# A gate vector cut in two around the out-projection, one set of square sums for two norms, and last slots by blocks of rows

## The chip, the cores and the metric

The kernel runs on one core of a Trainium2 chip. The metric is the device time of one execution in microseconds (us). The clocks in the profile are granted clocks of TensorE, as a share of 2.4 GHz: 1.00 is 2.4 GHz and 0.50 is 1.2 GHz.

## What is computed

Two transformer blocks in a row on one sequence of 256 tokens of width 1024, all in float32.

```python
def first_block(x, c, ...):
    cond = silu(c)
    for l in range(2):
        mod = cond @ w_ada[l] + b_ada[l]
        sh1, sc1, g1, sh2, sc2, g2 = split(mod, 6)
        h = rms_norm(x, g_norm_mix[l]) * (1 + sc1) + sh1
        z = h @ w_in[l]
        a_out = dsa_mixer(...)                    # sparse attention, 6 heads
        b_out = hgrn2_mixer(..., hgrn_out_norm)   # recurrence, norm per head, silu gate
        c_out = gmlp_mixer(...)                   # spatial products
        x = x + g1 * (concatenate([a_out, b_out, c_out]) @ w_out[l])
        h = rms_norm(x, g_norm_ffn[l]) * (1 + sc2) + sh2
        y = swiglu(h, ...) if l == 0 else moe_swiglu(h, ...)   # 8 experts, 2 per token
        x = x + g2 * y
    return rms_norm(x, g_final)

def second_block(x, ...):
    h = x + forgetting_attention(rms_norm_2(x, a_norm), ...)
    h = h + conv_ffn(rms_norm_2(h, f_norm[0]), ...)
    kv = shared_kv(h, ...)
    h = h + native_sparse_attention(rms_norm_2(h, b_norm), kv, ...)
    return h + conv_ffn(rms_norm_2(h, f_norm[1]), ...)
```

## The kernel before

**Weights.** SyncE (SP) streams all large weights in one fixed order, `ORDER`, through a ring of six buffers `raw` of 1 MB (L709). A slot is loaded when the slot six before it has been used. ScalarE copies a slot into `w_hi`, rounded (`split`, L877), and VectorE takes the rest into `w_lo` (L1853). TensorE makes three products for each one wanted: high by high, low by high and high by low (`three`, L1256 to L1258). ScalarE and VectorE run a few slots ahead of TensorE. The conditioning weights `ada` are the exception: TensorE uses them unsplit.

**Conditioning vectors.** Each of the twelve vectors takes four slots and 16 products on one row (`vector`, L1298), a row copy with its bias by ScalarE (`vec_row`, L1065), a broadcast over the partitions by TensorE (`over_rows`, L1308), and for most a copy into `mod` (`vec_over_rows`, L1073, counted by `vec_made`). In the order of use of a layer they are: scale and shift of the first norm, gate of the mixers (`first`), scale (`first + 1`) and shift (`first + 2`) of the second norm, and the gate of the FFN or of the experts (`6 * l + 5`). Bias rows come from GpSimd's (POOL's) queue (`next_bias`).

**Order.** Each engine has its own instruction stream, written out by hand in the order of the computation, with semaphores between them. For a layer of the first block it is: norm, in-projection, index scores and top 64 on VectorE while TensorE makes the vectors; attention (`attend`); recurrence in eight levels; its output in two banks (signal `o_out`, L1660 to L1662); the gate vector `vector(6 * l + 5)`; the transposes of the spatial weights (L1668); the spatial products (L1675); transposes of `mix` (L1332); out-projection; norm; FFN or experts. ScalarE copies the transposed spatial weights (L1137) before it takes the root of the recurrence's norm (L956).

**Out-projections and down-projections.** A slot of an out-projection holds four chunks of the contraction for 512 columns. TensorE goes over the chunks and, for each, over the two blocks of 128 rows. When a group of 512 columns is complete, VectorE adds both blocks into `X` (`into_residual`, L1870, L1963, L1965). The last down-projection slot of a dense FFN is used in the same way (`dense`). `square_sums` (L951) on ScalarE squares each block of `X`, `inv_rms` and `norm_rows` make the normed rows `H` (L1933, L1936), TensorE transposes them, ScalarE copies the columns into `xT_hi` (L943) and VectorE makes `xT_lo` (L1903).

**Experts.** The sum over experts is in `acc`; for each expert `scatter` (L1518) puts the rows back by a product and `take` (L2158) adds them, weighted. After the last expert all four engines that need it read the overflow word (more than 128 rows for an expert) and branch. Then `add_gated` (L1870, L2240) adds `acc` times the gate to `X`; one norm with `g_final` writes `X` (L2504), and a second with `a_norm_2` writes `H`.

**Fillers.** `turns(n)` (L1315) issues n products on TensorE whose results nobody reads: 12 before the transposes that follow the experts, 4 in each convolution layer, 5 before the shared keys, 9 before the compressed keys. In a convolution layer TensorE first transposes the taps (L1748) and ScalarE copies them (L1198) before its squares.

**The end.** When both blocks of `X` are complete, VectorE signals with a small copy (`beat`, L2020), and SP stores `X` in one DMA (L760).

## Time and profile before

| what | value |
|---|---|
| median of 3 runs (lowest, highest) | 2475.71 us (2468.77, 2479.25) |
| profiled execution, its own time | 2482.26 us |
| its span, first to last instruction | 2480.2 us |
| TensorE products busy | 2331.4 us, 94% |
| VectorE busy | 1838.7 us, 74% |
| ScalarE busy | 1330.6 us, 54% |
| moved by DMA | 584.43 MB, mean 236 GB/s |
| mean granted clock | 0.95 |

A busy TensorE is not TensorE at its peak, since its products overlap and their ends are modelled. A row of the timeline reads: start, duration, engine, line, operation, what it writes and reads, how many instructions are merged in the row, and in brackets the idle time of the engine before it and what ended that idle time. What matters for a joint is which engine arrives last.

### The profile page before, as it was taken

The numbers are of one execution on the slowest core, as the hardware profiler recorded it, in microseconds if no ns is written. First come the engines' busy times: TensorE is split into PE (matmuls) and PEld (weight loads), VectorE is DVE, ScalarE is ACT, GpSimd is POOL, SyncE is SP. The second block draws the span as 40 slices with busy tenths as digits, with TensorE's granted clock in tenths as the row PEclk, the third lists the DMA queues.
The fourth block names the chain that finished last, engine by engine and source line by source line (L and its number), as shares of the span: only waits on it lengthen the run. The fifth ranks groups of instructions, "written<-read, shape, count | busy, mean of one in ns | idle before, by whom it ended". The sixth has DMA issues, their size and how long they took to land.

```text
span 2480.2 us, 30703 instructions
## 1 busy us (share of the span) xinstructions
PE 2331.4 (94%) x12633; PEld 1916.2 (77%) x12633; DVE 1838.7 (74%) x2231; ACT 1330.6 (54%) x1335; POOL 34.2 (1%) x62
## 2 busy tenths in 40 slices
PE   7979999988899999999999999997989999888998
PEld 4666999657578888888888888875768997656998
DVE  4746564675778888888988888875747887765886
ACT  3332543442467777677777777763444433464432
...
GB/s 345 234 111 186 196 187 187 198 268 43 156 298 352 365 350 365 352 360 355 362 354 361 353 362 355 361 347 100 157 32 180 186 184 131 135 1 84 185 185 101
DMA packets 281266, 584.43 MB, mean 236 GB/s; under 512 B 12014, under 2 KB 86876, under 8 KB 280992
## 3 DMA queue, kind: packets, MB, share of 16 engines
...
HBM read 581.32 MB, written 1.05 MB: 235 GB/s over the span
## 4 chain that ended last, share of the span: by engine, by line
PE 85%; DVE 8%; ACT 4%; DMA 2%; issue 1%; DVEq 0%; POOL 0%; ACTq 0%; POOLq 0%
PE ps L1256 24%; PE ps L1258 24%; PE ps L1257 24%; PE ps L1298 2%; DVE w_lo L1853 2%; PE ps L1362 1%; DMA raw<-in_w_ada 1%; PE ps L1377 1%; PE ps L1619 1%; PE ps L1400 1%; ACT arena L973 1%; PE ps L1477 1%; DVE arena L2061 1%; DVE arena L1870 1%; PE ps L1636 1%
## 5 line engine op out<-in xcount | busy, mean ns | idle before, releaser
L877 ACT ACTIVATE w_hi<-raw 128x2048 fp32r<-128x2048 f32 x500 | 948.7, 1906 | 435.0 <-PE ps L1258 317.0
L1853 DVE TENSOR_TENSOR w_lo<-raw,w_hi 128x2048 fp32r<-128x2048 f32 x500 | 1117.3, 2272 | 25.6 <-ACT w_hi L877 23.6
L1256 PE MATMUL ps<-w_hi,xT_hi 128*128 128x512 f32 (+1 forms) x1408 | 553.9, 393 | 14.0 <-DVE w_lo L1853 5.8
L1257 PE MATMUL ps<-w_lo,xT_hi 128*128 128x512 f32 (+1 forms) x1408 | 546.4, 388 | 0.0
L1258 PE MATMUL ps<-w_hi,xT_lo 128*128 128x512 f32 (+1 forms) x1408 | 546.3, 388 | 0.0
L1256 PEld LDWEIGHTS ps<-w_hi,xT_hi 128*128 128x128 f32 x1408 | 270.4, 192 | 69.3 <-issue 8.1
L1258 PEld LDWEIGHTS ps<-w_hi,xT_lo 128*128 128x128 f32 x1408 | 270.1, 192 | 54.0
L1257 PEld LDWEIGHTS ps<-w_lo,xT_hi 128*128 128x128 f32 x1408 | 270.8, 192 | 50.7
L1256 PE MATMUL ps<-xT_hi,w_hi 128*128 128x256 f32 x1056 | 299.7, 284 | 4.7 <-DVE xT_lo L1903 4.7
L1257 PE MATMUL ps<-xT_lo,w_hi 128*128 128x256 f32 x1056 | 299.4, 284 | 0.0
L1258 PE MATMUL ps<-xT_hi,w_lo 128*128 128x256 f32 x1056 | 299.4, 283 | 0.0
L1256 PE MATMUL ps<-w_hi,aT_hi 128*128 128x512 f32 (+1 forms) x744 | 287.3, 386 | 2.2 <-DVE aT_lo L2179 1.4
L1257 PE MATMUL ps<-w_lo,aT_hi 128*128 128x512 f32 (+1 forms) x744 | 287.1, 386 | 0.0
L1258 PE MATMUL ps<-w_hi,aT_lo 128*128 128x512 f32 (+1 forms) x744 | 286.8, 385 | 0.0
L1256 PEld LDWEIGHTS ps<-xT_hi,w_hi 128*128 128x128 f32 x1056 | 203.2, 192 | 7.1 <-DVE w_lo L1853 3.1
L1257 PEld LDWEIGHTS ps<-xT_lo,w_hi 128*128 128x128 f32 x1056 | 203.3, 193 | 1.1
L1258 PEld LDWEIGHTS ps<-xT_hi,w_lo 128*128 128x128 f32 x1056 | 203.2, 192 | 0.0
L1256 PEld LDWEIGHTS ps<-w_hi,aT_hi 128*128 128x128 f32 (+1 forms) x744 | 137.6, 185 | 30.9 <-DVE aT_lo L2179 1.7
L1258 PEld LDWEIGHTS ps<-w_hi,aT_lo 128*128 128x128 f32 (+1 forms) x744 | 137.4, 185 | 28.6
L1257 PEld LDWEIGHTS ps<-w_lo,aT_hi 128*128 128x128 f32 (+1 forms) x744 | 137.5, 185 | 27.2
L1041 ACT ACTIVATE aT_hi<-arena 128x512 fp32r<-128x512 f32 x33 | 20.9, 632 | 178.4 <-DVE arena L2141 178.4
L1298 PE MATMUL ps<-raw,small 128*64 128x512 f32 x384 | 91.4, 627 | 3.1 <-DMA raw<-in_w_ada 3.1
...
## 6 DMA issues: line engine op xcount, KB each, us to landing
raw<-in_moe_w_gate SPq DMA_DIRECT2D x112, 1024.0 KB, 5.9
raw<-in_moe_w_up SPq DMA_DIRECT2D x112, 1024.0 KB, 5.4
raw<-in_moe_w_down SPq DMA_DIRECT2D x112, 1024.0 KB, 5.7
raw<-in_w_ada SPq DMA_DIRECT2D x48, 1024.0 KB, 7.8
raw<-in_f_w_up SPq DMA_DIRECT2D x44, 1024.0 KB, 5.0
raw<-in_f_w_down SPq DMA_DIRECT2D x22, 1024.0 KB, 5.1
raw<-in_w_in SPq DMA_DIRECT2D x20, 1024.0 KB, 7.9
raw<-in_a_w_in SPq DMA_DIRECT2D x12, 1024.0 KB, 5.2
```

What stands on the lines that cost most here:

```text
L877: act.activation(w_hi[:, k % HI, 0:size], raw[:, r, 0:size], ACT.Copy).then_inc(ring.w_hi_ready, 1)
L973: last = act.activation(x, x, ACT.Exp, bias=negmax[:, s % 4, h:h + 1], accum_out=rowsum[:, s % 4, h:h + 1])
L1256: pe.matmul(out_, lh, rh, start=start, stop=False)
L1257: pe.matmul(out_, lh, rl, start=False, stop=False)
L1258: return pe.matmul(out_, ll, rh, start=False, stop=stop)
L1298: last = pe.matmul(out_[HD * s:HD * s + HD, :], condT[:, 2 * q + c:2 * q + c + 1].to_broadcast([P, HD]), w[:, c, s, :], start=q == 0 and c ...
L1362: last = pe.transpose(ps[0:kw, 6 + u // 4, (u % 4) * P:(u % 4 + 1) * P], bufs[at.nth[i] % 3][:, x:x + kw], ident)
L1377: last = pe.matmul(ps[:, 4 * (1 - s % 2) + h % 2, (h // 2) * 256:(h // 2) * 256 + W], q(h), k(h), start=True, stop=True)
L1400: last = pe.matmul(out_[:, j * P:j * P + w], v[0 if shared else 2 * j + parity](c), Ts[s % 2][0:kw, x:x + w], start=at.first[i] and c == 0 ...
L1477: last = pe.transpose(ps[:, 2, j * P:(j + 1) * P], e_act[:, j * P:(j + 1) * P], ident)
L1619: last = pe.matmul(ps[:, 2 * (level % 2) + u // 4, (u % 4) * P:(u % 4 + 1) * P], h_LF[:, b, u // 2 * P:(u // 2 + 1) * P], const[:, e:e + P ...
L1853: dve.tensor_tensor(w_lo[:, k % RAW, 0:size], raw[:, k % RAW, 0:size], w_hi[:, k % HI, 0:size].bitcast(F32), ALU.subtract).then_inc(ring.w ...
```

## The change

The stream order becomes: one slot of the gate vector of the FFN (or experts) ahead of the out-projection, its other three slots (`ada05_rest`, `ada15_rest`) behind it. On TensorE one quarter of that vector stands after the spatial products and three after the out-projection. The scale of the second norm is broadcast after the spatial weights' transposes, and the shift after the out-projection, where `norm_rows` reads it from PSUM. The recurrence's output is normed with fewer steps behind `o_out`. Last slots are used block of rows by block of rows, with the signal `first_block` between. In the experts, what is summed before the last expert is folded into `X` early, and the squares of `X` and of `X` times `g_final` give both norms. The store is made in two parts. The fillers are not touched.

```diff
+        FIRST_PART = 1
         def linears():
             s = {}
             for l in range(2):
                 for v in range(6):
-                    s[f"ada{l}{v}"] = [(2, D, rows(a["w_ada"][l], 2 * q, 2, v * D, D)) for q in range(KC // 2)]
+                    slots = s[f"ada{l}{v}"] = [(2, D, rows(a["w_ada"][l], 2 * q, 2, v * D, D)) for q in range(KC // 2)]
+                s[f"ada{l}5"], s[f"ada{l}5_rest"] = slots[:FIRST_PART], slots[FIRST_PART:]
...
-        ORDER = ["ada01", "ada00", "in0", "ada02", "ada04", "ada03", "ada05", "out0", "ada11", "ffn0", "ada10", "in1",
-                 "ada12", "ada14", "ada13", "ada15", "out1", "moe",
+        ORDER = ["ada01", "ada00", "in0", "ada02", "ada04", "ada03", "ada05", "out0", "ada05_rest", "ada11", "ffn0", "ada10", "in1",
+                 "ada12", "ada14", "ada13", "ada15", "out1", "ada15_rest", "moe",
...
+        BY_BLOCK = ("out0", "out1", "fa_out", "nsa_out")
...
-        WIDE_BANK = [4, 2, 2, 2, 2, 6, 4, 2, 2, 2, 2, 6]
+        WIDE_BANK = [4, 2, 2, 4, 6, 6, 4, 2, 2, 4, 6, 4]
...
-            sp.wait_ge(result, got(result))
-            sp.dma_start(out[0].rearrange("(b p) n -> p b n", p=P), X[:, :, :]).then_inc(stored, 16)
-            sp.wait_ge(stored, 16)
+            for b in range(TB):
+                sp.wait_ge(result, got(result))
+                sp.dma_start(out[0, b * P:(b + 1) * P, :], X[:, b, :]).then_inc(stored, 16)
+            sp.wait_ge(stored, 16 * TB)
...
-                for i in range(6 * l + 2, 6 * l + 6):
+                for i in range(6 * l + 2, 6 * l + 5):
                     next_bias(i)
                 pool.wait_ge(ws_free, got(ws_free))
                 load(ws, a["gmlp_w_s"][l].rearrange("g t s -> t g s"), ld_ws)
                 load(bs_rows, a["gmlp_b_s"][l], ld_ws)
+                next_bias(6 * l + 5)
...
+            load(gain_n, a["a_norm_2"][0].partition_broadcast(P), ld_gain)
...
-            gain_row(a["a_norm_2"][0])
...
+                        vec_over_rows(5)
...
-                vec_over_rows(first + 1)
-                vec_over_rows(first + 2)
...
                 act.activation(bsT, ps[:, 1, 0:4], ACT.Copy).then_inc(ws_sb, 1)
+                vec_over_rows(first + 1)
                 root(stat_a[:, 0:12])
                 if l:
                     act.wait_ge(ld_first, 32)
                     act.activation(router_hi[:, :, :], router, ACT.Copy).then_inc(router_high, 1)
-                vec_row(6 * l + 5)
                 upto(BASE[f"out{l}"] + 1)
                 to_columns(3, bank=4)
                 linear(f"out{l}")
                 square_sums(X)
                 root(rstd)
-                vec_over_rows(6 * l + 5)
-                if l == 0:
+                vec_row(6 * l + 5)
+                if l:
+                    vec_over_rows(11)
+                else:
                     upto(BASE["ffn0"])
...
-            square_sums(X)
-            root(rstd)
-            square_sums(X)
-            root(rstd)
+            act.activation(stat_b[:, 8:9], ones[:, 0:1], ACT.Sqrt)
+            for b in range(TB):
+                for n_, src, squares in ((0, X, H), (2, acc, mix)):
+                    act.wait_ge(x_ready, got(x_ready))
+                    act.activation(squares[:, b, :], src[:, b, :], ACT.Square,
+                                   accum_out=stat_b[:, n_ + b:n_ + b + 1]).then_inc(sumsq_ready, 1)
+            root(stat_b[:, 0:4])
...
+                        if name in BY_BLOCK and i + part == len(slots) - 1:
+                            for k in range(nk):
+                                last = product(k, 0)
+                            last.then_inc(first_block, 1)
+                            for k in range(nk):
+                                last = product(k, 1)
+                        else:
+                            for k in range(nk):
+                                for b in range(blocks):
+                                    last = product(k, b)
                         last.then_inc(w_used, 1)
...
+                    bank = 0 if b and e == N_EXPERTS - 1 else 6
...
                 vector(first + 2)
-                pe.wait_ge(vec_made, 5 * l + 1)
-                over_rows(first + 1)
-                pe.wait_ge(vec_made, 5 * l + 2)
-                over_rows(first + 2)
                 pe.wait_ge(idx_taken, got(idx_taken))
-                pe.wait_ge(vec_made, 5 * l + 3)
+                pe.wait_ge(vec_made, 4 * l + 1)
+                pe.wait_ge(vec_rows, first + 3)
                 attend(dsa[l], att_bufs, att_T, [
...
-                vector(6 * l + 5)
                 pe.wait_ge(ws_masked, got(ws_masked))
                 for g in range(C_GROUPS):
                     pe.transpose(ps[:, 0, g * P:(g + 1) * P], ws[:, g, :], ident)
                 pe.transpose(ps[:, 1, 0:4], bs_rows, ident[0:4, 0:4]).then_inc(ws_tr, 1)
+                over_rows(first + 1)
                 pe.wait_ge(ws_sb, got(ws_sb, 2))
                 pe.wait_ge(v_normed, got(v_normed))
                 for b in range(TB):
...
                         last = pe.matmul(ps[:, 2 + b, g * HD:(g + 1) * HD], wsT[:, g, :], z[:, b, c:c + HD],
                                          start=True, stop=True)
                 last.then_inc(spatial, 1)
+                pe.wait_ge(vec_made, 4 * l + 2)
+                vector(6 * l + 5, 0, FIRST_PART)
                 to_columns(mix, 3, bank=4, blocks=False)
                 linear(f"out{l}")
+                over_rows(first + 2)
+                vector(6 * l + 5, FIRST_PART)
                 if l == 0:
                     vector(6)
-                over_rows(6 * l + 5)
+                else:
+                    over_rows(11)
                 to_columns(H)
                 if l == 0:
-                    dense(lambda: over_rows(6))
+                    dense(lambda: (over_rows(5), over_rows(6)))
                 else:
                     pe.wait_ge(router_low, 1)
+                    pe.wait_ge(vec_made, 7)
...
+            def norm_rows(shift=None):
                 for b in range(TB):
-                    last = dve.scalar_tensor_tensor(H[:, b, :], X[:, b, :], rstd[:, b:b + 1], scale, ALU.mult, ALU.mult)
-                    if adaptive:
+                    last = dve.scalar_tensor_tensor(H[:, b, :], X[:, b, :], rstd[:, b:b + 1],
+                                                    gain if shift is None else mod[:, 1, :], ALU.mult, ALU.mult)
+                    if shift is not None:
                         step(last)
-                        last = dve.tensor_tensor(H[:, b, :], H[:, b, :], mod[:, 0, :], ALU.add)
+                        h = H[:, b, :].rearrange("p (k n) -> p k n", k=2)
+                        if b == 0:
+                            dve.wait_ge(vec_wide, shift + 1)
+                        last = dve.tensor_tensor(h, h, ps[:, WIDE_BANK[shift]:WIDE_BANK[shift] + 2, :], ALU.add)
                     last.then_inc(rows_ready, 1)
...
+            def block_summed(name, b):
+                if b == 0:
+                    dve.wait_ge(first_block, got(first_block))
+                else:
+                    dve.wait_ge(w_used, BASE[name] + (len(SL[name]) if name in SL else 3 * N_GROUPS))
...
+            def fold(b):
+                tt(acc[:, b, :], acc[:, b, :], mod[:, 2, :], ALU.mult)
+                tt(X[:, b, :], X[:, b, :], acc[:, b, :], ALU.add)
+            def last_rows(to, final):
+                e = N_EXPERTS - 1
                 expert_rows(to)
                 for b in range(TB):
-                    take(to, N_EXPERTS - 1, b)
+                    bank = 0 if b else 6
+                    dve.wait_ge(to.scattered, got(to.scattered))
+                    dve.tensor_tensor(halved(acc[:, b, :]), ps[:, bank:bank + 2, :], halved(mod[:, 2, :]),
+                                      ALU.mult).then_inc(to.taken, 1)
+                    dve.wait_ge(to.taken, sent(to.taken))
+                    summed = dve.scalar_tensor_tensor(X[:, b, :], acc[:, b, :], gates[:, b, e:e + 1], X[:, b, :],
+                                                      ALU.mult, ALU.add)
+                    if not final:
+                        step(summed)
+                        continue
+                    summed.then_inc(x_ready, 1)
+                    dve.wait_ge(x_ready, sent(x_ready))
+                    dve.tensor_tensor(acc[:, b, :], X[:, b, :], gain, ALU.mult).then_inc(x_ready, 1)
...
+                    if e + 1 == N_EXPERTS and g in (2, 4):
+                        upto(k + 4 + 2, ring)
+                        fold(g // 2 - 1)
...
+                G = z[:, :, BG:BG + BD]
+                by_head = [P, TB, B_HEADS, HD]
+                def heads(x):
+                    return x.rearrange("p b (h d) -> p b h d", h=B_HEADS)
+                tt(heads(G), heads(G), onorm.unsqueeze(1).unsqueeze(1).to_broadcast(by_head), ALU.mult)
                 dve.wait_ge(o_out, got(o_out))
-                for b in range(TB):
-                    step(dve.tensor_copy(h_O[:, b, :], ps[:, 6 + b, 0:BD]))
+                found = ps[:, 6:8, 0:BD]
+                step(dve.tensor_copy(h_O[:, :, :], found))
                 tt(h_sq, h_O, h_O, ALU.mult)
                 step(dve.tensor_reduce(stat_a[:, 0:12], h_sq.rearrange("p b (h d) -> p (b h) d", d=HD), AX.X, ALU.add))
-                inv_root(stat_a[:, 0:12], stat_a[:, 0:12], HD)
-                o4 = h_O.rearrange("p b (h d) -> p (b h) d", d=HD)
-                tt(o4, o4, stat_a[:, 0:12].unsqueeze(2).to_broadcast([P, 12, HD]), ALU.mult)
-                tt(o4, o4, onorm.unsqueeze(1).to_broadcast([P, 12, HD]), ALU.mult)
-                dve.wait_ge(gate_silu, got(gate_silu))
-                tt(mix[:, :, BD:2 * BD], h_O, z[:, :, BG:BG + BD], ALU.mult)
+                def gated():
+                    tt(h_O, h_O, G, ALU.mult)
+                inv_root(stat_a[:, 0:12], stat_a[:, 0:12], HD, gated)
+                o_rstd = stat_a[:, 0:12].rearrange("p (b h) -> p b h", b=TB)
+                tt(heads(mix[:, :, BD:2 * BD]), heads(h_O), o_rstd.unsqueeze(3).to_broadcast(by_head), ALU.mult)
...
+            upto(AFTER + 1)
+            dve.wait_ge(sumsq_ready, got(sumsq_ready, 4))
+            first_rstd, both_rstd = stat_b[:, 0:2], stat_b[:, 2:4]
+            ts(first_rstd, first_rstd, 1.0 / D, ALU.mult, EPS, ALU.add)
+            step(dve.reciprocal(first_rstd, first_rstd))
+            stt(both_rstd, both_rstd, 1.0 / D, first_rstd, ALU.mult, ALU.mult)
+            ts(both_rstd, both_rstd, EPS, ALU.add)
+            step(dve.reciprocal(both_rstd, both_rstd))
+            dve.tensor_tensor(both_rstd, both_rstd, first_rstd, ALU.mult).then_inc(root_in, 1)
+            dve.wait_ge(root_in, sent(root_in))
+            dve.wait_ge(root_out, got(root_out))
             for b in range(TB):
-                dve.scalar_tensor_tensor(X[:, b, :], X[:, b, :], rstd[:, b:b + 1], gain, ALU.mult,
-                                         ALU.mult).then_inc(x_ready, 1)
-                dve.wait_ge(x_ready, sent(x_ready))
-            beat().then_inc(gain_free, 1)
-            dve.wait_ge(gain_free, sent(gain_free))
-            upto(AFTER + 1)
+                dve.scalar_tensor_tensor(H[:, b, :], acc[:, b, :], both_rstd[:, b:b + 1], gain_n, ALU.mult,
+                                         ALU.mult).then_inc(rows_ready, 1)
+                dve.wait_ge(rows_ready, sent(rows_ready))
+            for b in range(TB):
+                ts(X[:, b, :], acc[:, b, :], first_rstd[:, b:b + 1], ALU.mult)
...
+                made = x_ready if name == "conv0" else result
                 for b in range(TB):
                     x = X[:, b, :].rearrange("p (k n) -> p k n", k=2)
-                    dve.tensor_tensor(x, x, sums(b), ALU.add).then_inc(x_ready, 1)
-                    dve.wait_ge(x_ready, sent(x_ready))
+                    block_summed(name, b)
+                    dve.tensor_tensor(x, x, sums(b), ALU.add).then_inc(made, 1)
+                    dve.wait_ge(made, sent(made))
```

## Rows read from the trace of the kernel before

**Rows 1.** Windows: us, PE, PEld, DVE, ACT, POOL busy, clock, DMA share, GB/s.
```profile
1302.00:1364.00 62.00, 62.00 (x282) 51.22 (x281) 54.74 (x32) 44.96 (x30) 0.00 (x0) 1.00 1.00 362
...
660.20:672.70 12.50, 5.01 (x22) 3.42 (x21) 9.46 (x15) 4.96 (x10) 1.84 (x4) 0.64 0.30 99
```

**Rows 2.** Timeline, head of the first attention, ScalarE and TensorE.
```profile
129.06 1.19 ACT L1065 ACTIVATE vec<-ps 32x512 f32<-32x512 f32 x2 [7.27 <-PE ps L1298]
...
131.35 1.13 PE L1308 MATMUL ps<-vec,small 64*128 64x512 f32 x4 [1.28 <-ACT arena L1073]
...
133.69 0.94 PE L1377 MATMUL ps<-arena 64*128 64x128 f32 x12 [1.22 <-ACT arena L1073]
```

**Rows 3.** Timeline, end of the first layer's recurrence.
```profile
195.31 9.08 PE L1298 MATMUL ps<-raw,small 128*64 128x512 f32 x32
...
195.48 1.15 DVE L2403 COPY arena<-ps 128x384 f32<-128x384 f32 x2 [0.64 <-PE ps L1662]
...
206.03 0.96 DVE L1870 TENSOR_TENSOR arena<-arena,small 128x768 f32<-128x768 f32 x1 [6.95 <-ACT small L956]
...
210.67 2.39 PE L1332 MATMUL ps<-const,mix 128*128 128x128 f32 x10 [2.79 <-DVE mix L2421]
```

**Rows 4.** Windows of 2 us around the first out-projection's start.
```profile
197.00:199.00 2.00, 2.00 (x8) 0.70 (x6) 1.90 (x4) 0.00 (x0) 0.00 (x0) 0.50 0.00 0
...
209.00:211.00 2.00, 0.33 (x2) 0.33 (x3) 1.84 (x5) 1.72 (x1) 0.00 (x0) 0.65 1.03 422
...
213.00:215.00 2.00, 1.70 (x5) 1.34 (x5) 2.00 (x5) 2.00 (x3) 0.00 (x0) 0.50 0.59 201
```

**Rows 5.** Timeline, from the first out-projection to the FFN.
```profile
236.77 7.09 PE L1298 MATMUL ps<-raw,small 128*64 128x512 f32 x32
...
245.72 1.22 DVE L1936 TENSOR_TENSOR Z<-Z,arena 128x1024 f32<-128x1024 f32 x1
...
247.00 1.09 PE L1332 MATMUL ps<-const,Z 128*128 128x128 f32 x8 [1.05 <-DVE Z L1936]
...
250.94 0.55 PE L1256 MATMUL ps<-xT_hi,w_hi 128*128 128x256 f32 x1 [2.85 <-DVE xT_lo L1903]
```

**Rows 6.** Timeline, second layer: recurrence's end, then the norm's columns.
```profile
619.21 1.15 DVE L2403 COPY arena<-ps 128x384 f32<-128x384 f32 x2 [1.05 <-PE ps L1662]
...
634.12 2.40 PE L1332 MATMUL ps<-const,mix 128*128 128x128 f32 x10 [2.93 <-DVE mix L2421]
...
671.16 2.07 ACT L943 ACTIVATE xT_hi<-ps 128x512 fp32r<-128x512 f32 x4 [5.09 <-PE ps L1332]
```

**Rows 7.** Timeline, end of the experts.
```profile
1684.79 1.28 DVE L2158 SCALAR_TENSOR_TENSOR Z<-ps,small,Z 128x1024 f32<-128x1024 f32 x1 [2.24 <-PE ps L1518]
...
1690.47 12.50 PE L1315 MATMUL ps<-const 128*128 128x512 f32 x24 [5.79 <-issue]
...
1700.87 2.61 DVE L1933 SCALAR_TENSOR_TENSOR Z<-X,small,Z 128x1024 f32<-128x1024 f32 x2 [1.16 <-DMA Z<-in_a_norm]
...
1702.81 1.91 PE L1332 MATMUL ps<-const,Z 128*128 128x128 f32 x16
```

**Rows 8.** Timeline, norms after the FFN, the first attention output, the first convolution.
```profile
449.39 1.13 PE L1308 MATMUL ps<-vec,small 64*128 64x512 f32 x4 [1.85 <-ACT vec L1065]
...
1869.14 0.32 ACT L1198 ACTIVATE arena<-ps 128x176 f32<-128x176 f32 x1 [3.83 <-PE ps L1748]
...
2065.30 2.48 DVE L2583 TENSOR_TENSOR X<-X,ps 128x1024 f32<-128x1024 f32 x2 [1.44 <-PE ps L1258]
...
2071.90 1.09 PE L1332 MATMUL ps<-const,Z 128*128 128x128 f32 x8 [2.35 <-DVE Z L1933]
```

**Rows 9.** Timeline, the store.
```profile
2475.84 0.39 SPq L760 DMA_DIRECT2D out<-X  x1
```

**Rows 10.** DMA issues: bytes and median us to landing.
```profile
out<-X SPq DMA_DIRECT2D x1, 1024.0 KB, 4.0
...
raw<-in_a_w_in SPq DMA_DIRECT2D x1, 64.0 KB, 2.3
```

111 lines of the change are left out of this document (64 added, 47 removed).

## Prediction

> **What bounds the kernel now.** I read the windows of the span first. In the expert stage TensorE is busy in all 62.00 us of a window, with 282 products at 0.22 us each and the granted clock at 1.00, while the DMA share is 1.00 and VectorE has 7 us to spare; between the second out-projection and the router, 660.2 to 672.7, TensorE is busy for 5.01 of 12.50 us at a clock of 0.64 [rows 1]. The reader is to see two kinds of stage: long streams of products, which this change hardly touches, and the joints between them, where TensorE waits in turn for VectorE and ScalarE. So I went on to the timeline of each joint that the diff touches, and read which instruction starts the next stream and what that instruction waited for. A joint pays only where the shortened engine is the last to arrive.
>
> **1. Head of each attention.** At 129.06 ScalarE copies the shift's bias row, and then come a row copy, a broadcast product (1.13 us), another copy and the wait for it, until scores start at 133.69 [rows 2]. Only the first copy stays: 129.06 + 1.19 + 0.05 = 130.30. VectorE had its mask ready before, since its next work was these scores. That is 3.4 us a layer; I take 3.2, as ScalarE's table load may now be met, and 2 x 3.2 = **6.4** (bounds 0 and 6.8).
>
> **2. From the recurrence to the out-projection.** VectorE begins at 195.48, is stopped for 6.95 us by the square root, and lets TensorE begin its transposes at 210.67, 15.2 us in all [rows 3]. The root waited because ScalarE's queue had the copies of the transposed spatial weights ahead of it, and those transposes stood behind 9.08 us of gate vector on TensorE [rows 3]. Take the vector away and the 6.95 us go. Three edits act on VectorE too: the norm gain is multiplied in ahead (0.96 + 0.03 us leaves the chain, but only 0.64 us was idle there, so 0.35 comes back), two copies of 1.15 us together become one of 0.96, and the product with the gate fills the root's latency. 15.2 - 6.95 - 0.99 + 0.35 - 0.2 = 7.4 us: rows ready near 202.9, 7.7 earlier. On TensorE there now stand transposes, the scale's broadcast, the spatial products and one quarter of the vector (9.08 / 4 = 2.3, at 1.2 GHz nearer 3.4). ScalarE copies the broadcast (1.02) before the root, still before the root is asked for at 199.3. The quarter may end some 0.5 us after the rows, so I take 7.2. In the second layer the chain runs from 619.21 to 634.12 and also holds 0.25 us for the router's split [rows 6]; I take 7.1. Together **14.3** (bounds 10 and 19, the latter if TensorE, no longer idle, starts the projection at 2.4 GHz).
>
> **3. After the first out-projection.** Before, TensorE did one vector, 7.09 us or 1.77 a quarter, and a broadcast; the rows of the second block came at 246.95, and the FFN started 14.1 us after the projection's end at 236.8 [rows 5]. Now there stand a broadcast (1.13), three quarters (5.3) and the vector (7.1) = 13.5 us, while by the early first block VectorE's rows are there at 8.7 instead of 10.1. So TensorE is late next: two sets of transposes at 1.09 and the pipeline of the columns, 0.7 + 1.5 us, give 13.5 + 1.1 + 2.2 = 16.7. That is **-2.6**. The two broadcasts inside the FFN are one more than before, **-1.1** on a TensorE without gaps. The SP queue must now bring the three vector slots and then the FFN's: the first FFN slot is asked for at 4.7 us, behind two of some 3 us each, lands near 10 and has both its splits (1.9 and 2.3) by 14.5, under the 13.5 of products. Cost bounds 2.5 and 6.
>
> **4. FFN's end.** The first block's gating and sum, 2 x 1.24 us, move under the last products. But the vector of the next layer's shift, 7.1 us on TensorE, keeps its place, and after it TensorE stood idle for only 1.85 us until ScalarE had copied the row at 449.39 [rows 8]. That copy itself takes 1.19 and its signal 0.06, so only **0.6** is won.
>
> **5. Router.** Block by block VectorE is 1.45 us earlier. TensorE has a broadcast, 5.3 us of vector, 1.25 of row copy, and 1.1 of broadcast: free at 8.8 us, both transposes done by 11, against 12.2. ScalarE's column copy, 10.9 us after the projection before [rows 6], comes near 10.3: **0.6** (bounds -0.8 and 1.5). Two expert slots that VectorE split during the projection are now split in the gap before the gather, 2 x 2.3 in 4.8 us: nothing as long as that gap stands, 1 us if not.
>
> **6. Experts.** Two folds of 2 x 1.24 us use VectorE's spare 7 us per window [rows 1]. Nothing, at worst 2. At POOL the gain row moves ahead of the layer parameters and lands long before its reader.
>
> **7. End of the experts.** The norms really lose about 7 us: two rounds of squares become one, and rows would be ready near 1695. But TensorE's next products are twelve filler products, 12.50 us from 1690.47, and the transposes begin at 1702.81 exactly behind them, with VectorE's first rows at 1702.2 [rows 7]. The fillers start 4.4 us after the last sum is signalled (1684.79 + 1.28), the read of the overflow word. The diff leaves all twelve in place. The last signal now comes at 1686.36, since two more operations stand ahead of it: **-0.3** instead of +7 (bounds -2 and +7).
>
> **8. Attention outputs (fa_out and nsa_out).** The first block is summed early, but ScalarE is stopped by the wait for the convolution's transposes until 1869.14, and the squares start behind that copy at 1869.49 [rows 8]. **0**.
>
> **9. First convolution to the shared keys.** No such wait: squares follow the sums at 2065.30, 1.24 us each, and the second block's is all that is left. TensorE was idle for 2.35 us before its transposes [rows 8], so its fillers don't bind. **+1.25**.
>
> **10. The store.** The two sums end 1.24 us after the last product and the beat is gone: issue at 2474.5 instead of 2475.84 [rows 9], 1.35. On SP 64 KB land in 2.3 and 1024 KB in 4.0 us [rows 10], so 512 KB in about 3.1: 0.9 more (bounds 0 and 1.7). **+2.25**.
>
> Sum: 6.4 + 14.3 - 3.7 + 0.6 + 0.6 + 0 - 0.3 + 0 + 1.25 + 2.25 = **21.4 us**. The profiled execution took 2482.26 us for a span of 2480.2, so it would take 2460.9. It lies 6.55 us above the median of the runs, 2475.71, so the median becomes **2454.3**.
>
> **Rivals.** *The vectors cost more where they went* (13%). The three quarters after each projection need slots freed only late; before, the queues were full between the projection and the FFN. If each layer loses 5 us more there, 10 to 12 us remain: 2465. For it speaks that TensorE is the late engine there already; against it that the slots in question have 10 us to land.
>
> *The fillers don't bind* (8%). If the last product of the experts is signalled so much earlier that the fillers start early, 7 us come on top: 2447. Against it stands the unchanged wait for the last sum.
>
> *The cold projection, slower* (5%). The 9.08 us of vector raised the clock: it is 0.50 at 197 to 199, and TensorE is busy throughout. After the idle wait it is 0.65 at 209 to 211 and 0.50 in the first products of the projection, 1.2 GHz [rows 4]. If with the vector gone a projection ran cold throughout, some 90 of its 96 products would take twice the 0.22 us, 20 us more, 40 in both: 2454 + 40 = 2494, slower by 18. The point is the number of cold products: from 97 more of them (21.4 / 0.22) the gain is gone. Against it, the clock had risen while TensorE was busy, and the joint now has fewer idle gaps, not more. The Trainium skill, TensorE: Matmul & The Clock Gate, "HAM oscillation", holds that idle gaps send the array back to 1.2 GHz and that work must bridge them; by that rule removing the filler speaks for this rival. The drop at 209 agrees.
>
> *It doesn't do what it says* (6%): the first block's signal comes no earlier, or the root stays behind something else; 8 us or less, about 2468.
>
> **The numbers.** The forecast has 68%; its own range is 2446 to 2463. Bounds of the terms and the first two rivals reach from 2443 to 2467, which leaves out under 2 in 10. A measurement of this kernel tells 0.5%, 12.4 us, from no change. Faster by more: nearly all of the forecast, all of the second rival, a third of the first: 80%. Within: 15%. Slower: 5%.
>
> **What would show it.** Scores right after one row copy; the first product of each out-projection 17 us after the recurrence turns to 10 after it; FFN start 16 to 17 us after the projection; rows of the norm ready near 1695 in old time, with VectorE idle for 7 us until fillers end; ScalarE's squares after fa_out unmoved; two stores, the last issued 1.4 us after the last product. Wrong would be: fillers that start earlier, a projection at a clock of 0.50 beyond its first dozen products, or TensorE waiting for DMA among the three quarters.

## The result and the profile after

The changed kernel takes 2450.98 us, the median of 5 runs (2448.5 to 2453.25). The kernel before took 2477.98 beside it (5 runs). The ratio is 0.9895, with a 95% interval of 0.9879 to 0.9911: the medians differ by 27.0 us, where 21.4 were forecast, and the interval of the ratio is 22.1 to 30.0 us. The profiled execution took 2450.4 us. Three lines of its page:

```profile
span 2448.6 us, 30711 instructions
...
PE 2318.8 (95%) x12633; PEld 1909.2 (78%) x12633; DVE 1841.5 (75%) x2233; ACT 1328.3 (54%) x1333; POOL 34.2 (1%) x62
...
PEclk9988999997999999999999999998979999879999
```

The busy times hardly moved. I read the timeline of both kernels from joint to joint (end of one stream of products to the first product of the next), and made this table of it. "After again" is the same changed kernel in another group of runs (experiment 5).

| stretch, us | before | after | after again |
|---|---|---|---|
| start to the end of the first in-projection | 104.11 | 104.86 | 105.52 |
| first scores, attention, recurrence (layer 1) | 91.26 | 88.57 | 89.58 |
| recurrence's end to first projection | 18.00 | 10.02 | 11.43 |
| first projection | 23.47 | 23.66 | 22.07 |
| projection's end to FFN | 14.10 | 17.01 | 17.02 |
| FFN | 189.58 | 190.58 | 190.58 |
| FFN's end to in-projection | 16.99 | 16.41 | 16.42 |
| attention, recurrence (layer 2) | 95.72 | 89.90 | 90.28 |
| recurrence's end to second projection | 18.06 | 10.03 | 10.04 |
| second projection | 23.40 | 22.08 | 22.08 |
| projection's end to router | 12.48 | 11.59 | 11.58 |
| router to the last expert's scatter | 1006.48 | 1006.57 | 1007.73 |
| scatter to the attention's in-projection | 26.46 | 27.98 | 27.42 |
| that projection, attention, its output | 163.10 | 159.83 | 163.02 |
| to the first convolution | 9.23 | 9.08 | 9.09 |
| first convolution to the shared keys | 10.20 | 8.78 | 8.78 |
| shared keys to the end of nsa_out | 201.12 | 197.82 | 198.32 |
| to the second convolution | 9.22 | 9.07 | 9.07 |
| last product to the end | 7.14 | 4.40 | 4.40 |

The last expert's scatter is taken at its first product (1679.18 us before, 1657.01 after), so the stretch behind it holds the scatter too. The in-projection of layer 2 (65.5 to 66.0) and the convolutions (187.3 in all three) are left out. The sum of the four stages with attention or a recurrence in them fell from 551.2 to 536.1 us, 6.6 of it by the edit; the rest of the span fell from 1929.0 to 1912.5.

**Head of the attention.** Timeline of after, ScalarE and TensorE, first layer; it answers to [rows 2].

```profile
129.97 1.19 ACT L1077 ACTIVATE vec<-ps 32x512 f32<-32x512 f32 x2 [7.44 <-PE ps L1323]
...
131.30 0.94 PE L1402 MATMUL ps<-arena 64*128 64x128 f32 x12 [1.38 <-ACT vec L1077]
```

From the row copy to the scores it is 1.33 us, for 4.63 before; in the second layer 1.33 for 4.63 too.

**Recurrence to projection.** Timeline of after, the three engines; it answers to [rows 3].

```profile
192.66 0.96 DVE L1911 TENSOR_TENSOR Z<-Z,lp 128x768 f32<-128x768 f32 x1
193.65 0.96 DVE L2493 COPY arena<-ps 128x768 f32<-128x768 f32 x1
194.41 2.08 PE L1333 MATMUL ps<-vec,small 64*128 64x512 f32 x4
194.52 0.60 ACT L1147 ACTIVATE arena<-ps 128x512 f32<-128x512 f32 x1 [4.45 <-PE ps L1703]
197.09 0.96 DVE L1911 TENSOR_TENSOR arena<-arena,Z 128x768 f32<-128x768 f32 x1
197.46 0.20 ACT L967 ACTIVATE small<-small 128x12 f32<-128x12 f32 x1
198.09 0.96 DVE L1911 TENSOR_TENSOR mix<-arena,small 128x768 f32<-128x768 f32 x1
198.53 1.94 PE L1323 MATMUL ps<-raw,small 128*64 128x512 f32 x8
200.75 1.31 PE L1357 MATMUL ps<-const,mix 128*128 128x128 f32 x10 [0.28 <-DVE mix L2512]
203.45 0.64 PE L1270 MATMUL ps<-w_hi,xT_hi 128*128 128x512 f32 x1 [1.39 <-DVE w_lo L1894]
```

VectorE goes from one instruction to the next from 192.66 to 200.69. The root (L967) runs at 197.46, under the product with the gate, and the 6.95 us of idle time are gone. The quarter of the vector ends at 200.47, just before VectorE's rows. What is late next is the product's own `w_lo`: VectorE splits it in 2.29 us after the rows.

**Behind the first projection.** Timeline of after; it answers to [rows 5].

```profile
228.09 12.24 PE L1323 MATMUL ps<-raw,small 128*64 128x512 f32 x56
...
234.51 1.22 DVE L1982 TENSOR_TENSOR Z<-Z,ps 128x1024 f32<-128x1024 f32 x1
...
239.07 1.91 ACT L888 ACTIVATE w_hi<-raw 128x2048 fp32r<-128x2048 f32 x1 [4.37 <-DMA raw<-in_ffn_w_gate]
240.26 1.97 PE L1357 MATMUL ps<-const,Z 128*128 128x128 f32 x16
241.08 2.29 DVE L1894 TENSOR_TENSOR w_lo<-raw,w_hi 128x2048 fp32r<-128x2048 f32 x1 [5.16 <-ACT w_hi L888]
...
244.12 0.36 PE L1270 MATMUL ps<-xT_hi,w_hi 128*128 128x256 f32 x1 [1.90 <-DVE xT_lo L1945]
```

TensorE is the late engine: rows are ready at 235.73, 8.6 us after the projection's end at 227.11, and the seven slots of vector end at 240.3. The FFN's first slot lands only at 239.07, 12.0 us after the projection; its split ends at 243.37, just before the columns.

**End of the experts.** Timeline of after; it answers to [rows 7].

```profile
1668.79 13.54 PE L1340 MATMUL ps<-const 128*128 128x512 f32 x24 [8.03 <-issue]
1670.88 2.60 DVE L2609 SCALAR_TENSOR_TENSOR Z<-Z,small 128x1024 f32<-128x1024 f32 x2 [0.34 <-ACT small L967]
1682.16 1.91 PE L1357 MATMUL ps<-const,Z 128*128 128x128 f32 x16
1683.46 2.06 ACT L954 ACTIVATE xT_hi<-ps 128x512 fp32r<-128x512 f32 x4 [12.68 <-PE ps L1357]
1684.16 2.48 DVE L1945 TENSOR_TENSOR xT_lo<-ps,xT_hi 128x512 fp32r<-128x512 f32 x4 [9.09 <-ACT xT_hi L954]
```

The rows of the norm are complete at 1673.48. ScalarE then stands idle for 12.68 us and VectorE for 9.09, behind fillers that end at 1682.33.

**Attention output and store.** Timeline and DMA issues of after; they answer to [rows 8, 9, 10].

```profile
1845.22 0.32 ACT L1212 ACTIVATE arena<-ps 128x176 f32<-128x176 f32 x1 [3.83 <-PE ps L1789]
1845.44 1.05 ACT L962 ACTIVATE Z<-X 128x1024 f32<-128x1024 f32 x1
```

```profile
2444.27 1.22 DVE L2689 TENSOR_TENSOR X<-X,ps 128x1024 f32<-128x1024 f32 x1 [1.57 <-PE ps L1272]
```

```profile
out<-X SPq DMA_DIRECT2D x2, 512.0 KB, 2.6
```

The squares still stand behind the copy of the taps. The second half of the store starts when the sum of 1.22 us is made; a half lands in 2.6 us.

### The profile page after: what moved, and what is told of

It is laid out like the page before. It is cut to its first block, busy times and chain, and to the rows that moved or that the text cites. A ratio compares the mean times of both kernels' runs of the same rounds, so it can differ in the third digit from the quotient of the medians.

```text
span 2448.6 us, 30711 instructions
## 1 busy us (share of the span) xinstructions
PE 2318.8 (95%) x12633; PEld 1909.2 (78%) x12633; DVE 1841.5 (75%) x2233; ACT 1328.3 (54%) x1333; POOL 34.2 (1%) x62
## 4 chain that ended last, share of the span: by engine, by line
PE 86%; DVE 7%; ACT 4%; DMA 2%; issue 1%; POOL 0%; DVEq 0%; ACTq 0%; POOLq 0%
PE ps L1270 24%; PE ps L1271 24%; PE ps L1272 24%; PE ps L1323 2%; DMA raw<-in_w_ada 1%; PE ps L1402 1%; PE ps L1387 1%; DVE w_lo L1894 1%; PE ps L1654 1%; ACT arena L984 1%; PE ps L1514 1%; DVE arena L1911 1%; PE ps L1425 1%; PE ps L1671 1%; DVE arena L2116 1%
## 5 line engine op out<-in xcount | busy, mean ns | idle before, releaser
L1270 PE MATMUL ps<-w_hi,xT_hi 128*128 128x512 f32 (+1 forms) x1408 | 552.7, 393 | 16.0 <-DVE w_lo L1894 7.3
L1323 PE MATMUL ps<-raw,small 128*64 128x512 f32 x384 | 86.5, 598 | 3.4 <-DMA raw<-in_w_ada 3.4
```

The lines of the kernel that those rows point to most:

```text
L1270: pe.matmul(out_, lh, rh, start=start, stop=False)
L1323: done = pe.matmul(out_[HD * s:HD * s + HD, :], condT[:, 2 * q + c:2 * q + c + 1].to_broadcast([P, HD]), w[:, c, s, :], start=q == 0 and c ...
```

## The experiments

Each is an edit of the changed kernel. All kernels of a group were timed against the kernel before on the same chip (medians of before: 2474.99, 2478.99, 2475.54 and 2480.1 us).

### 1. Three fillers

```diff
-            turns(12, 5)
+            turns(3, 5)
```

> The changed kernel with 3 filler products after the experts where it has 12. Theory (the fillers hide the norms' gain): the fillers end near 1671.7, before the rows (1672.2 and 1673.5 in the changed kernel), so the first product of the attention's in-projection comes near 1676.5 to 1677.5 where it came at 1684.99; the median falls by 6 to 8 us from 2451.0, to 2443 to 2445, 0.986 to 0.987 of the kernel before. Rival (the fillers pay for themselves by the clock): the first product comes that early too, but the products after it stay at 0.50 so long that at the end of the in-projection less than 3 us of the 8 are left: 2448 to 2451. Second rival (something else releases the transposes): the first product stays within 2 us of 1684.99.

2448.61 us, ratio 0.9894 (0.9875 to 0.9912). The timeline, TensorE:

```profile
1672.43 5.06 PE L1340 MATMUL ps<-const 128*128 128x512 f32 x6 [7.85 <-issue]
1677.32 1.91 PE L1357 MATMUL ps<-const,Z 128*128 128x128 f32 x16
1680.15 0.25 PE L1270 MATMUL ps<-w_hi,xT_hi 128*128 128x16 f32 x1 [0.92 <-DVE xT_lo L1945]
```

This execution is 3.8 us later at the scatter (1660.83 for 1657.01); from there to the first product it takes 19.32 us for 27.98. So the fillers did hide the norms' gain: 8.7 us. But the median fell by little or nothing, where the theory had 0.986 to 0.987. Its number is the first rival's, but not its place: the in-projection behind took 74.85 us, as in the changed kernel (74.87), so it is not there that the 8.7 us were lost. The second rival is out.

### 2 and 3. The old end of the experts, with 12 and with 3 fillers

```diff
-                        last_rows(main_pass, True)
+                        last_rows(main_pass)      # two sums, then add_gated
-            root(stat_b[:, 0:4])
+            square_sums(X); root(rstd); square_sums(X); root(rstd)
...
-            turns(12, 5)
+            turns(3, 5)        # in experiment 3 alone
```

> The changed kernel with the end of the experts as it was before: no folds, two sums a block and then the gate, two rounds of squares and two norms; 12 fillers. Theory (the fillers bind in both kernels): the first product of the attention's in-projection comes within 1.5 us of the changed kernel's 1684.99, and the median within 2 us of 2451.0. Rival (the single set of square sums is worth its 7 us): first product near 1692, median near 2458, 0.992 of the kernel before.

> The end of the experts as before and 3 fillers for 12. Theory: now the rows bind. They are ready some 15 to 16 us after the last sum is taken (1662.9 to 1664), near 1679 to 1680, so the first product comes near 1683 and the median lies 0 to 2 us below that with the old end and 12 fillers, and 5 to 7 us above that with the new end and 3 fillers. Rival (the norms are not what the transposes wait for): the first product comes within 2 us of the one with the new end and 3 fillers.

With 12: 2451.05 us, 0.9901 (0.9885 to 0.9917); scatter to first product 26.45 us. With 3: 2458.99 us, 0.9941 (0.9918 to 0.9963); 26.00 us. With the old end the rows come only 0.45 us before the end of twelve fillers; with the new end and 3 fillers the joint is 19.32 us. The change of the norms is worth 6.7 us (5.9 to 7.1 over the four profiles with 3 fillers, 18.92 to 20.07), and with 12 fillers none of it: 27.98 or 27.42 against 26.45 even. Those fillers begin 0.4 to 0.5 us later after the scatter's start (11.78 and 11.90 us for 11.40), and take 13.54 and 12.85 us for 12.38. Of the 24 instructions of twelve fillers the first start 0.85 us apart, at 1.2 GHz, and the rest 0.43: some seven are slow in the changed kernel, some four in experiment 2. The idle time ahead does not decide how many: after 8.12 us of it twelve fillers took 12.41 us (experiment 7), after 4.48 us 13.49 (experiment 8).

The medians do not follow: 2 and 3 should differ by half a microsecond and differ by 8, where the theory had 0 to 2 the other way. The profiled execution of 2 took 2461.45 us, the slowest of its six and 10 us above their median.

### 4. Without blocks of rows

```diff
-                        if name in BY_BLOCK and i + part == len(slots) - 1:
+                        if False:
...
-                if b == 0:
-                    dve.wait_ge(first_block, got(first_block))
+                if b == 0:
+                    dve.wait_ge(w_used, ...)      # the whole slot
```

> The changed kernel with the last slots in the old order (chunk by chunk, both blocks of rows), and both blocks taken after the slot. Theory by the steps of the prediction: first projection 0, since TensorE is late there; FFN's end 0.6, router 0.6, attention outputs 0, first convolution to the shared keys 1.25, the store 1.2: about 3.7 us more than 2451.0, 2454.7, 0.991 of the kernel before. Rival (the orders cost or give nothing that lasts): within 1 us. Rival (each joint pays its 1.2 to 1.45 us): 8 us, 2459, 0.993.

2458.31 us, 0.9936 (0.9918 to 0.9953). Its joints, against the changed kernel: FFN's start 16.98 (17.01), FFN's end 17.05 (16.41), router 12.15 (11.59), convolutions 9.23 and 9.22 (9.08, 9.07), shared keys 9.97 (8.78), the end 5.63 (4.40). That is 0.64 + 0.56 + 0.15 + 0.15 + 1.19 + 1.23 = 3.9 us where 3.7 were expected, and the terms are where the theory had them, but for the 0.15 twice where it had none. By the ratios the kernel is some 10 us slower than the changed one, 6 more than its joints say: 2458.31 us is the second rival's number, but not for its reason: of the joints only the shared keys and the end pay the 1.2 us that it gave to each.

### 5. The changed kernel again

> The changed kernel again, unchanged, beside the others of this group. Theory (the stages in which TensorE waits for small work, attention, recurrence and sparse attention, differ from execution to execution by the clock, the dense stages do not): the dense stages repeat to 0.1 us (the convolutions 187.3, the FFN 190.6), the first attention output stage (first product of the in-projection to the end of the out-projection, 159.8 before) may be anywhere from 156 to 166. Rival (those stages belong to the edit): it repeats 159.8 within 1 us.

2452.14 us, 0.9893 (0.9877 to 0.9909). The FFN and the convolutions repeat to 0.04 us, the experts to 1.2, the start with the first in-projection to 0.7. The stage from the attention's in-projection to its output took 163.02 us for 159.83. One window over that whole stage, in this kernel, in the changed kernel's first profile, in experiment 4 and in experiment 7, in that order, one fence each (columns as in [rows 1]):

```profile
1687.72:1850.74 163.02, 146.20 (x711) 120.92 (x712) 90.46 (x163) 73.42 (x117) 1.81 (x3) 0.86 0.33 107
```

```profile
1684.99:1844.82 159.83, 144.44 (x711) 119.67 (x712) 90.56 (x163) 73.33 (x117) 1.82 (x3) 0.87 0.34 110
```

```profile
1686.93:1843.25 156.32, 139.36 (x711) 115.59 (x712) 89.80 (x162) 73.33 (x117) 1.81 (x3) 0.91 0.34 112
```

```profile
1689.13:1858.13 169.00, 153.84 (x711) 127.17 (x712) 90.57 (x163) 73.46 (x117) 1.81 (x3) 0.81 0.32 104
```

The same 711 products and the same 90 us of VectorE take 156 to 169 us, and the order of the times is the order of the clocks, 0.91 to 0.81. Experiment 4 changes the order of the products in the last slot of this stage, where the out-projection takes 22.05 us for 22.08; no other of these edits touches it.

### 6. Taps first, three fillers

```diff
-            turns(12, 5)
+            turns(3, 5)
...
+            conv_taps(0)                 # wait for the load, four transposes
             linear("fa_out")
```

and likewise ahead of `nsa_out`.

> The changed kernel with 3 fillers for 12 and with the transposes of the convolution's taps ahead of the attention's out-projections, so that ScalarE has copied them before its squares. Theory (step 8: ScalarE's squares stood behind that copy): the squares of the second block start when its sum is made, 0.87 us earlier, and the joints from the out-projections to the convolutions take 8.2 us where they took 9.08, twice. With the fillers' 8.7 that is 10 us less than the changed kernel of the same group, 0.4%. Rival (something else is late there, the fillers of the convolution layer for one): 9.08 stays. Rival for the fillers: the joint is 8.7 shorter again but the median within 2 us of the changed kernel's, because the attention behind runs longer at 1.2 GHz.

2454.7 us, 0.9905 (0.9889 to 0.9921), where 10 us less than the changed kernel were expected. The joints to the convolutions are 8.26 and 8.25 us: step 8's reason stands. But the edit put a new wait into the stream. TensorE at the attention's output:

```profile
1817.86 0.62 PE L1760 MATMUL ps<-const,arena 44*128 44x44 f32 x4 [4.16 <-DMA arena<-in_f_conv_b]
1818.41 0.79 PE L1270 MATMUL ps<-w_hi,xT_hi 128*128 128x512 f32 x1
1819.00 0.63 PE L1271 MATMUL ps<-w_lo,xT_hi 128*128 128x512 f32 x1
```

The taps are loaded only when VectorE is through with the attention (`conv_free`). TensorE waits 4.16 us, and the out-projection behind starts at 1.2 GHz: 24.22 us for 22.1. At `nsa_out` it waits 4.13 us, and the projection takes 24.55. That is 12.9 us in all.

### 7. The whole vector ahead of the projection

```diff
-        FIRST_PART = 1
+        FIRST_PART = 4
```

> The changed kernel with the whole gate vector ahead of the out-projection, behind the spatial products (FIRST_PART 4), nothing behind it. Theory: TensorE is the late one on both sides. Ahead of each projection 3 quarters are added, 5.3 us at 2.4 GHz and up to 10 at 1.2: from the recurrence's end to the first product 15.5 to 20 us where it was 10 to 12. Behind the first projection 17.0 falls by 5.3 at most, to 11.7, but VectorE's rows and the columns need 13.5, so 13.5. Behind the second 11.6 falls to about 10. Sum: slower than the changed kernel by 6 to 14 us. Rival (VectorE sets the start of the projection, as its rows are ready only 10 us after): 11 to 12 us stays ahead of the projection, and the kernel gets faster by 3 to 5.

2460.44 us, 0.9922 (0.9907 to 0.9936). TensorE in the first layer, and in the second:

```profile
201.67 7.09 PE L1323 MATMUL ps<-raw,small 128*64 128x512 f32 x32
208.69 1.31 PE L1357 MATMUL ps<-const,mix 128*128 128x128 f32 x10
...
604.33 1.11 PE L1702 MATMUL ps<-const,arena 128*128 128x128 f32 x4 [2.45 <-DVE arena L2481]
607.58 3.67 PE L1710 MATMUL ps<-Z,arena 128*128 128x64 f32 x16
611.18 9.59 PE L1323 MATMUL ps<-raw,small 128*64 128x512 f32 x32
```

Two joints with the same instructions: 13.05 us in the first layer, 19.88 in the second. Behind them 11.89 (17.01) and 12.22 (11.59). With the clock up, three slots ahead cost 3.0 us and give 5.1 back behind the first projection. In the second layer the joint is 9.8 us longer than the changed kernel's 10.03, but 2.45 of that is a wait for VectorE's masked weights (L2481). The products of the recurrence's output had run at 2.4 GHz there, 0.39 us each for 0.63 in the first layer, so TensorE came to the transposes before VectorE did. What the slots cost at 1.2 GHz is better read from their own time: 9.59 us for 32 instructions here and 3.68 for 8 in experiment 5, 5.9 us more. The clock over the second joint:

```profile
604.00:616.30 12.30, 11.97 (x37) 6.37 (x39) 8.52 (x15) 3.37 (x6) 1.11 (x2) 0.50 0.10 38
616.30:621.77 5.47, 5.47 (x32) 2.33 (x29) 2.29 (x1) 2.64 (x3) 0.00 (x0) 1.00 0.95 320
```

The theory's 15.5 to 20 ahead holds for one layer of the two. From the recurrence's end to the FFN's end, and in the second layer to the router, the kernel is 3.7 us shorter than the changed one in the first layer and 10.4 longer in the second, 6.7 in all; the ratios say 7, inside the 6 to 14 of the theory.

### 8. The vector in its old place

```diff
+                vector(6 * l + 5, 0, FIRST_PART)      # FIRST_PART = 4
                 pe.wait_ge(ws_masked, got(ws_masked))
```

> As e7, but the vector stands where it stood in the kernel before, ahead of the transposes of the spatial weights. Theory (step 2: the root stood behind the copies of the transposed spatial weights, and these behind the vector): VectorE is idle for 5 to 7 us again before it scales the recurrence's output, and the joint takes 16 to 17.5 us, nearly the 18.0 of before. The gap to e7 in this joint is what the order alone is worth, gap to the changed kernel what the whole step is worth, 6 to 7.5 us a layer. Rival (the gain came from VectorE's shortened chain, not from the vector's place): 11 to 13 us.

In this kernel the broadcast of the scale goes to the bank in which the vector still waits, so the gate gets other values and the experts another load; only what lies ahead of the experts is read, where the work is the same. (Its whole execution, 3458.9 us, tells nothing here.) VectorE and ScalarE, first layer:

```profile
194.61 0.96 DVE L1911 TENSOR_TENSOR arena<-arena,Z 128x768 f32<-128x768 f32 x1
...
198.79 0.60 ACT L1147 ACTIVATE arena<-ps 128x512 f32<-128x512 f32 x1 [11.20 <-PE ps L1704]
200.78 0.20 ACT L967 ACTIVATE small<-small 128x12 f32<-128x12 f32 x1
201.08 0.96 DVE L1911 TENSOR_TENSOR mix<-arena,small 128x768 f32<-128x768 f32 x1 [5.52 <-ACT small L967]
```

The 5.52 us of idle time are back, for the reason that step 2 names: ScalarE's root stands behind its copy of transposes that stand behind 8.09 us of vector. The joints take 16.46 and 17.56 us. So of the 8 us of the step 6.4 and 7.5 are where the vector stands: behind the spatial products, and with three quarters of it behind the projection. The other 1.5 and 0.5 are VectorE's shorter chain and, in the first layer, 1.0 us of a vector that ran at a higher clock (8.09 us for 9.08). The order alone, this kernel against experiment 7, is 3.4 us in the first layer, and -2.3 in the second, where experiment 7 has its wait of 2.45 us.

A joint is not the whole account, for what leaves it comes back behind the projection. Time from the end of the recurrence, in the first layer to the end of the FFN, in the second to the router:

| us | before | vector in its old place (8) | after | again |
|---|---|---|---|---|
| layer 1: joint, projection, behind it, FFN | 245.1 | 242.3 | 241.3 | 241.1 |
| layer 2: joint, projection, behind it | 54.0 | 53.6 | 43.7 | 43.7 |

The vector's new place is worth 1.0 to 1.2 us in the first layer, since the stretch behind the projection grows from 11.90 to 17.02 us there and the FFN starts at 1.2 GHz (190.58 us for 189.08). In the second layer the stretch behind the projection did not grow (11.59 us, and 12.34 with the vector in its old place), and the place is worth 9.9.

### 9 and 10. Twenty fillers, and three again

> The changed kernel with 20 fillers for 12. The joint from the experts to the attention's in-projection must get 8 x 0.43 = 3.5 us longer, 31 us for 27.5 to 28. Theory (filler products are paid back by the clock somewhere behind the joint: with 3 of them the joint was 8.7 us shorter and the median was not): the median stays within 2 us of the changed kernel's 2451 to 2452, 0.989 to 0.990 of the kernel before, and the mean granted clock is 0.958 or above. Rival (the clock behind the joint has nothing to do with the fillers, and the medians with 3 fillers were chance): 3 to 4 us slower, 2455, 0.991, clock no higher than with 12.

> The changed kernel with 3 fillers again. Theory (paid back by the clock): joint 19.3 us for 27.5 to 28, median within 3 us of the changed kernel's, 0.988 to 0.9905 of the kernel before, and a mean granted clock of 0.955 in most executions where 12 fillers gave 0.958. Rival (chance): 0.986 of the kernel before and a clock of 0.957 or more.

Twenty: 2462.0 us, 0.9936 (0.9914 to 0.9958); scatter to first product 34.26 us, as 20 fillers take 19.85 us. My 0.43 us for one was too small: `turns` issues two instructions for each, so that one costs 0.86 us at 2.4 GHz. The joint grew by 6.3 to 6.8 us, and by the ratios the kernel is 10 slower, which neither the theory nor the rival had. Three again: 2447.79 us, 0.9882 (0.986 to 0.9904), joint 20.07, which is the theory's number. Between these two kernels of one group the joint differs by 14.19 us and the median by 14.2: from 3 to 20 fillers nothing is paid back.

The kernel with 12 lies some 5 us below the line between them, about the half width of one interval. Whether the clock pays for fillers up to 12 these runs leave open. The pairs that differ in 12 or 3 fillers alone (the changed kernel with 1 and 10, and 2 with 3) speak for it: with 3 the mean granted clock of the runs is lower (0.955 and 0.956 for 0.959 and 0.958; with the old end 0.951 for 0.957), and the kernel is 5 to 10 us slower than its joints say. Against it stands that with 20 the clock is 0.957 and no gain is seen. The theory falls for the step from 12 to 20 alone.

### 11. Two slots ahead, taps first

`FIRST_PART = 2` and the taps as in experiment 6, with 12 fillers.

> The changed kernel with 12 fillers, the convolution's taps transposed ahead of the attention's out-projections, and two of the vector's four slots ahead of the layers' out-projections, two behind. Theory: the taps give 0.83 us twice. Of the second slot 1.8 us lies ahead of the projection and 1.8 less behind it; where TensorE has its full clock ahead of the projection it stood idle for 1.4 to 1.7 us there, so 10.0 becomes 10.2 to 10.5, and behind it 17.0 becomes 15.2; where it is at 1.2 GHz the second slot costs 3.7 ahead, 11.4 becomes 15. So 3 us less than the changed kernel with the clock up in the first layer, none or 2 more with it down. Rival (TensorE is never late ahead of the projection): 10 to 11 us in both layers, 15.2 behind, 4 to 5 us less.

2459.12 us, 0.9938 (0.9916 to 0.9959). Ahead of the projections 9.92 and 10.04 us, behind them 14.65 (17.01) and 10.70 (11.59), FFN 189.09 (190.58, its start no longer at 1.2 GHz). The joints gave all they should, but by the ratios the kernel is 11 us slower than the changed one, where the theory had 3 less. Against it stand the waits for the taps, 4.1 and 3.9 us, and 2.1 and 2.5 us of a cold `fa_out` and `nsa_out`; all of these lie in the four stages, 552.7 us for 536.1.

### 12. Three edits together

`FIRST_PART = 2`, 3 fillers, and the taps between the two halves of the out-projections:

```diff
-            linear("fa_out")
+            linear("fa_out", between={0: lambda: conv_taps(0)})
```

> The changed kernel with three edits that earlier runs price apart: 3 fillers for 12, two of the vector's slots ahead of the out-projections, and the transposes of the taps between the two halves of the attention's out-projections, where their load has long landed (ahead of the projections TensorE waited 4.1 and 3.9 us for it). Theory (the joints add up): after the experts 8 us less than the changed kernel, behind the first projection 2.4, behind the second 0.9, FFN 1.5, at the convolutions 2 x 0.83 less 2 x 0.44 for transposes that now stand in a stream of products; ahead of the projections 0 with the clock up and 3.6 more with it down, and attention output stages with their 22.1 us again. Sum 13.6, 2438, 0.984 of the kernel before; with the clock down in both layers 2445, 0.987. Rival (the medians do not follow the joints, because kernels differ in the time their attention stages spend at 1.2 GHz): the joints as said, the median at 2448 or above, 0.988.

2448.57 us, 0.9879 (0.985 to 0.9907). The profiled execution has the shortest span of all, 2441.5 us, and is 5 us below the median of its runs. Joints: experts 19.03, ahead of the projections 13.95 (the clock down) and 10.03, behind them 14.50 and 10.70, FFN 189.10, convolutions 8.37 and 8.25, no wait for the taps. The rest of the span is 1900.0 us, 12.5 below the changed kernel's. The median is the rival's: some 4 us below the changed kernel by the ratios, inside their intervals. No version was shown to beat the change.

All kernels, one profiled execution each: "four stages" are the two stretches of attention and recurrence, the attention with its projections, and shared keys to `nsa_out`. Experiment 8 is left out, since its experts have other work.

| kernel | four stages, us | rest of span, us | ratio of the medians |
|---|---|---|---|
| before | 551.2 | 1929.0 | 1 |
| after / again | 536.1 / 541.2 | 1912.5 / 1913.9 | 0.9895 / 0.9893 |
| 1, 10: three fillers | 539.4 / 543.4 | 1907.8 / 1905.5 | 0.9894 / 0.9882 |
| 2: old end | 541.5 | 1918.1 | 0.9901 |
| 3: old end, three fillers | 544.8 | 1910.0 | 0.9941 |
| 4: no blocks of rows | 530.6 | 1920.5 | 0.9936 |
| 6: taps first, three fillers | 544.6 | 1907.2 | 0.9905 |
| 7: whole vector ahead | 547.0 | 1917.3 | 0.9922 |
| 9: twenty fillers | 539.3 | 1920.5 | 0.9936 |
| 11: two slots ahead, taps first | 552.7 | 1902.4 | 0.9938 |
| 12: three edits | 541.5 | 1900.0 | 0.9879 |

## Why the prediction was right

The forecast said 2454.3 us and the median is 2451.0. The mechanisms held, and the edited joints come near their sum; that the total is so near rests in part on errors that cancel (steps 7 and 8 against 2, 5 and 10), and by the profiles most of what it gave beyond the forecast lies in stages that the change doesn't edit. By the steps, forecast then measured (after, and after again where it differs):

- **1**, heads of the attention: 6.4; 3.3 + 3.3 = 6.6.
- **2**, recurrence to projection: 14.3; 8.0 + 8.0 = 16.0, again 6.6 + 8.0 = 14.6. Over the nine profiles with a quarter ahead the joints are 10.0 to 14.7 us, mean 11.8 and 10.9: 13.4 on average. Experiment 8 shows the cause. The bound of 19 stood for projections that start at 2.4 GHz, and most did: they took 22.1 us for 23.4, with no 2.79 us of idle time left ahead of the transposes. That is 1.1 to 2.7 us that the sum lacked, and with it the step gives 17.1 and 17.3.
- **3**, behind the first projection: -2.6; -2.9. TensorE is late, as said; the FFN's slot lands at 12.0 and not near 10, and its split then ends with the columns. The broadcast in the FFN: -1.1; -1.0.
- **4**: 0.6; 0.6. **5**: 0.6; 0.9.
- **6**: 0; -0.1, again -1.2. The two expert slots split in the gap before the gather cost nothing: TensorE is idle for 2.01 us there and was for 2.08. The first group of products is 1.6 us longer all the same. Its window of after and of before, below, has the same 74 products and TensorE busy throughout, at a clock of 0.91 for 1.00; it is the clock, and in the first profile the experts behind make up for it.
- **7**: -0.3; -1.5 and -1.0. Experiments 1 to 3 show the mechanism whole: fillers hide 6.7 us. Of the 1.5 us 0.5 is a later start of the fillers, 0.25 of it the two more operations that the forecast named, and 1.0 is that more of them ran at 1.2 GHz (13.54 us for 12.50; 12.85 in the second profile).
- **8**: 0; 0.3, twice 0.15. The copy of the taps holds the squares, as experiments 6 and 12 show by taking it away.
- **9**: 1.25; 1.4. **10**: 2.25; 2.74, as a half lands in 2.6 us and not 3.1.

The windows for step 6, after and before:

```profile
666.89:685.10 18.21, 18.21 (x74) 14.91 (x75) 15.42 (x16) 11.25 (x7) 0.00 (x0) 0.91 0.70 249
```

```profile
689.22:705.84 16.62, 16.62 (x74) 13.74 (x75) 15.34 (x16) 11.25 (x7) 0.00 (x0) 1.00 0.75 273
```

Outside the four stages this gives 15.0 forecast and 16.5 measured, after 0.75 us that the unedited start lost. Inside them the edit gives 6.6. The profiled executions differ by 31.6 us, so 8.5 more come from stages in which nothing was edited (3.4 by the second profile). That is the term that the forecast did not have at all, and experiment 5 shows what it is: the granted clock in stages of small products. With one profile of the kernel before, no run shows how much of the 8.5 us is the change and how much chance.

Of the rivals, the vectors cost 0.3 us beyond the sum of step 3, and the fillers bound. The cold projection was not seen whole: the first products of one projection ran at 1.2 GHz in the first profile, as before. Windows of 2 us of after, which answer to [rows 4]:

```profile
194.00:196.00 2.00, 2.00 (x7) 0.68 (x5) 1.93 (x3) 0.66 (x2) 0.00 (x0) 0.50 0.00 0
...
202.00:204.00 2.00, 0.61 (x3) 0.45 (x3) 2.00 (x3) 2.00 (x4) 0.00 (x0) 0.91 0.87 285
204.00:206.00 2.00, 2.00 (x6) 1.55 (x5) 2.00 (x3) 2.00 (x2) 0.00 (x0) 0.50 1.00 401
206.00:208.00 2.00, 2.00 (x8) 1.63 (x7) 2.00 (x2) 0.62 (x1) 0.00 (x0) 0.73 0.16 66
```

TensorE was busy for 0.61 of 2.00 us there, waiting for `w_lo`, then fell to 0.50 for about 3 us. In eight of the nine profiles that projection took 22.0 to 22.1 us instead. Removing the vector did not cool the projections; it took away the larger gap. The rule that the forecast cited from the Trainium skill, TensorE: Matmul & The Clock Gate, "HAM oscillation", is that idle gaps send the array back to 1.2 GHz, and the trace agrees (before, the clock was at 0.65 in the window of the 2.79 us of idle time, [rows 4]); the 40 us of the rival that leaned on it did not come.

**What stays open.** Against the changed kernel, the ratios of experiments 1, 3, 4, 7 and 9 to 12 lie 3 to 15 us above what the rest of their span says; those of 2 and 6 lie 3 and 4 us below (in 6 and 11 the waits for the taps and the two cold projections, 12.9 and 12.6 us, are counted with it). Some of that is more than the scatter of runs of one kernel (the changed kernel's ten lie between 2448.5 and 2456.88), but an interval of a ratio is 4 to 7 us wide to each side. The mean granted clock of their runs is lower, 0.951 to 0.957, for 0.959 and 0.958 in the changed kernel's two groups. I take it that the changed kernel is lucky in how its small-work stages meet the clock, by some 5 us, and that this is the excess over the forecast; that is argued, not shown. Which part of the order decides it, its twelve fillers for one, no run tells apart.
